# A transformer step whose last expert pair reaches the output sums through a one-hot product on TensorE

## What is computed

```python
def hier_moe(h, ...):
    ...
    g_idx = jnp.argmax(glog, axis=-1)              # 1 of 4 groups
    ...
    top_v, top_i = lax.top_k(elog_g, TOP_K)        # 2 of its 8 experts
    gate = jax.nn.softmax(top_v, axis=-1) * g_w[:, None]
    ...
    # expert e: (silu(x @ w_gate[e]) * (x @ w_up[e])) @ w_down[e], D 1024, FF 512
...
x = x + hier_moe(rms_norm(x, lw["ln_ffn"]), ...)
...
y_prompt = rms_norm(yp, final_norm_g)
y_sample = rms_norm(ys, final_norm_g)
```

## Time and profile before

| | us |
|---|---|
| median of three runs | 1164.77 |
| lowest, highest | 1164.1, 1165.12 |
| the profiled execution | 1165.38 |
| its span (first to last instruction) | 1163.6 |
| PE busy in it | 1032.4 |
| DVE, ACT, POOL busy | 458.5, 186.1, 113.1 |

### The profile page before, as it was taken

How to read it: one execution, slowest core, us unless ns; L and a number is a source line. 1 busy time by engine, 2 the same in 40 slices (tenths; PEclk the granted TensorE clock), 3 DMA queues, 4 the chain that set the end, 5 groups by cost and what they waited for, 6 DMA issues and landing times.

```text
span 1163.6 us, 11497 instructions
## 1 busy us (share of the span) xinstructions
PE 1032.4 (89%) x4528; PEld 540.7 (46%) x4528; DVE 458.5 (39%) x770; ACT 186.1 (16%) x486; POOL 113.1 (10%) x167
## 2 busy tenths in 40 slices
PE   6999999999999999999998699987876889887880
PEld 3577744555445446777656343333332233333320
DVE  4169645563664024013227743322222233322224
ACT  0156233433113101012101000000000000000001
POOL 1200001132016000000000010010000000100002
PEclk9999999999999999999998699999989899989995
DMA  8221130312233433212085599999999999999977
GB/s 254 73 73 54 45 123 1 134 52 82 74 108 103 177 145 145 73 57 89 1 355 200 220 397 427 427 427 426 428 427 426 422 427 427 426 427 427 413 297 251
DMA packets 56548, 277.50 MB, mean 238 GB/s; under 512 B 13360, under 2 KB 15280, under 8 KB 44336
## 3 DMA queue, kind: packets, MB, share of 16 engines
q1 hardware_dynamic: 43648, 256.01, 54.7%
q10 hardware_dynamic: 7808, 11.32, 2.7%
q0 software_dynamic: 5040, 9.45, 2.2%
HBM read 273.34 MB, written 18.61 MB: 251 GB/s over the span
## 4 chain that ended last, share of the span: by engine, by line
PE 69%; DMA 18%; DVE 6%; SPq 4%; issue 2%; ACT 0%; POOL 0%; ACTq 0%; DVEq 0%; POOLq 0%
PE bank L497 23%; DMA arena<-in_exp_w_down_dram 15%; PE bank L485 13%; PE bank L882 12%; PE bank L872 6%; SPq L1089 4%; PE bank L501 2%; PE bank L747 2%; PE score_pair L721 2%; PE bank L635 1%; DVE arena L1675 1%; DMA arena<-expert_rows 1%; PE score_pair L551 1%; PE bank L585 1%; DMA arena<-in_w_in_dram 1%
## 5 line engine op out<-in xcount | busy, mean ns | idle before, releaser
L497 PE MATMUL bank<-arena 128*128 128x512 f32 x640 | 285.0, 599 | 2.6 <-DMA arena<-in_w_in_dram 1.9
L882 PE MATMUL bank<-arena 128*64 128x512 f32 x1024 | 238.3, 622 | 38.5 <-issue 35.2
L497 PEld LDWEIGHTS bank<-arena 128*128 128x128 f32 x640 | 119.7, 191 | 147.0 <-issue 145.5
L882 PEld LDWEIGHTS bank<-arena 128*64 128x64 f32 x1024 | 83.4, 143 | 190.6 <-issue 189.4
L485 PE MATMUL bank<-arena 128*128 128x288 f32 x640 | 156.1, 406 | 0.0
L872 PE MATMUL bank<-arena 128*64 128x512 f32 x512 | 119.5, 621 | 26.6 <-DMA arena<-in_exp_w_down_dram 19.5
L485 PEld LDWEIGHTS bank<-arena 128*128 128x128 f32 x640 | 121.4, 190 | 33.8 <-issue 0.4
L1298 ACT ACTIVATE arena<-bank 128x512 f32<-128x512 f32 (+6 forms) x135 | 61.7, 493 | 378.3 <-PE bank L497 112.5
L872 PEld LDWEIGHTS bank<-arena 128*64 128x64 f32 x512 | 39.9, 142 | 95.1 <-issue 83.5
L1521 ACT ACTIVATE arena<-bank,arena 128x512 f32<-128x512 f32 x17 | 11.7, 687 | 428.3 <-PE bank L882 404.4
L2045 DVE SCALAR_TENSOR_TENSOR arena<-bank,arena 128x512 f32<-128x512 f32 x34 | 25.5, 751 | 109.8 <-PE bank L872 102.8
(11 more groups left out here) (295 smaller groups left out, 928.1 us busy)
## 6 DMA issues: line engine op xcount, KB each, us to landing
arena<-in_exp_w_gate_dram SPq DMA_DIRECT2D x30, 2048.0 KB, 33.0
arena<-in_exp_w_up_dram SPq DMA_DIRECT2D x30, 2048.0 KB, 37.7
arena<-in_exp_w_down_dram SPq DMA_DIRECT2D x28, 2048.0 KB, 34.7
arena<-in_w_in_dram SPq DMA_DIRECT2D x7, 2048.0 KB, 8.5
out_dram<-arena SPq DMA_DIRECT2D x4, 1024.0 KB, 10.5
arena<-in_w_mem_k_dram SPq DMA_DIRECT2D x2, 2048.0 KB, 10.3
arena<-in_w_mem_v_dram SPq DMA_DIRECT2D x2, 2048.0 KB, 8.6
arena<-in_w_out_dram SPq DMA_DIRECT2D x2, 2048.0 KB, 12.7
```

Source lines behind the costliest of these rows:

```text
L497: ins = mm(b[:, :], x, w[:, k, :], start=k == 0, stop=k == KC - 1)
L882: ins = mm(bank[own, :], xgT[:, k, own], w[j][:, k, :], start=k == 0, stop=k == KC - 1)
```

## The change

- POOL's scatter of the last pair (15) is gone. In its place POOL writes the numbers 0 to 575 into every partition (`iota`).
- DVE keeps for each slot of the last pair its token number (`last_tok`), and ahead of pair 15's drains compares the numbers with it: `hot_last`, 128 slots x 576 tokens, is 1 where the slot belongs to the token. It does not tell first from second expert.
- PE sums in PSUM. `place_last` multiplies `hot_last` of a tile by the drained rows of the last pair, which puts each row at its token; `add_loaded` adds the two loaded rows of each token by products with the identity. There are two banks for each tile (`summed`), the fifth tile taking those of the first again.
- ACT's square and DVE's scaling read these banks; DVE's sum is gone.
- The rows of `y_dram` that belong to slots of the last pair are no longer written, so all of `y_dram` is zeroed at the start: SP waits for POOL's constants and writes it from the zeroed `Vbd` in four DMAs, and `spread_v(0)` waits for them.
- SP issues all ten row loads, behind the final gain, and waits only for the scatters up to pair 14. ACT issues none. `yg` moves to parts that pair 15 does not use.

```diff
@@ -114,7 +114,8 @@
         ints = ctx.enter_context(nc.sbuf_tensor("ints", [P, 256], I32))
-        banks = [ctx.enter_context(nc.psum_tensor(f"bank{i}", [P, 512], F32)) for i in range(6)]
+        bank_pairs = [ctx.enter_context(nc.psum_tensor(f"banks{2 * i}", [P, 2, 512], F32)) for i in range(3)]
+        banks = [bank_pairs[i // 2][:, i % 2, :] for i in range(6)]
         pair = ctx.enter_context(nc.psum_tensor("score_pair", [P, 2, 512], F32))
@@ -216,7 +217,11 @@
-        yg = [[area(1024 * (2 * t + k), 1024) for k in range(2)] for t in range(NT)]
+        ROWS = 28672
+        yg = [[area(ROWS + 1024 * (2 * t + k), 1024) for k in range(2)] for t in range(NT)]
+        count_i = area(ROWS + 10240, TOK, dt=I32)
+        count = area(ROWS + 10240 + TOK, TOK)
+        hot_last = area(ROWS + 10240 + 2 * TOK, TOK)
         gfin = xg[1]
@@ -337,6 +342,7 @@
         ocol = fixed(4)
+        last_tok = fixed(1)
@@ -403,11 +409,14 @@
         over_done = sem("over_passes_done")
+        y_zero, count_ready, hot_last_ready = sem("y_rows_zeroed"), sem("token_count_ready"), sem("last_one_hot_ready")
+        f_full = sem("tokens_summed")
         gf_ld = sem("final_gain_loaded")
         yg_ld = [sem(f"y_rows_loaded{t}") for t in range(NT)]
-        fsum, fssq, frstd, fin_ready = (sem(f"final_{n}") for n in ("sum", "ssq", "rstd", "ready"))
+        fssq, frstd, fin_ready = (sem(f"final_{n}") for n in ("ssq", "rstd", "ready"))
         fin_st = sem("final_stored")
+        summed = [bank_pairs[0], pair, bank_pairs[1], bank_pairs[2], bank_pairs[0]]
         A = PsumRing(banks[0:3], a_full, a_free)
@@ -978,6 +987,37 @@
                     turn_rows(SP_, xg_rows[(i + 1) % 3])
+            pe.wait_ge(hot_last_ready, 1)
+
+            def place_last(t, half):
+
+                t0, rows = TILES[t]
+                mm(summed[t][0:rows, half, :], hot_last[:, t0:t0 + rows], yS[(PAIRS - 1) % 2][:, 512 * half:512 * (half + 1)],
+                   start=True, stop=False, skip_group_check=True)
+
+            def add_loaded(t):
+
+                rows = TILES[t][1]
+                pe.wait_ge(yg_ld[t], 32)
+                for half in range(2):
+                    for k in range(2):
+                        ins = mm(summed[t][0:rows, half, :], ident[0:rows, 0:rows], yg[t][k][0:rows, 512 * half:512 * (half + 1)],
+                                 start=False, stop=k == 1, skip_group_check=True)
+                ins.then_inc(f_full, 1)
+
+            for half in range(2):
+                pe.wait_ge(SP_.y_cp, 2 * PAIRS - 1 + half)
+                for t in range(2):
+                    place_last(t, half)
+            for t in range(2, SAMPLE):
+                for half in range(2):
+                    place_last(t, half)
+            for t in range(SAMPLE):
+                add_loaded(t)
+            pe.wait_ge(fin_ready, 1)
+            for half in range(2):
+                place_last(SAMPLE, half)
+            add_loaded(SAMPLE)
@@ -1004,6 +1044,10 @@
             sp.dma_start(cvN, a["cache_diff_v"][0, 0].rearrange("t h d -> t (h d)")).then_inc(ldcache, 16)
+            sp.wait_ge(pool_c, 2)
+            y_flat = y_dram.rearrange("(p r) n -> p (r n)", p=P)
+            for c in range(4):
+                sp.dma_start(y_flat[:, 2304 * c:2304 * (c + 1)], area(OZ, 2304)).then_inc(y_zero, 16)
             for u in range(2, 6):
@@ -1114,9 +1158,10 @@
             sp.wait_ge(y_st[0], 16 * (PAIRS // 2))
-            sp.wait_ge(y_st[1], 16 * (PAIRS // 2))
+            sp.wait_ge(y_st[1], 16 * (PAIRS // 2 - 1))
             for t, (t0, rows) in enumerate(TILES):
-                sp.dma_start(yg[t][0][0:rows, :], y_dram[t0:t0 + rows, :]).then_inc(yg_ld[t], 16)
+                for k in range(2):
+                    sp.dma_start(yg[t][k][0:rows, :], y_dram[TOK * k + t0:TOK * k + t0 + rows, :]).then_inc(yg_ld[t], 16)
             for t, (t0, rows) in enumerate(TILES):
@@ -1171,6 +1216,7 @@
                 if h == 0:
+                    po.wait_ge(y_zero, 64)
                     po.wait_ge(a_free, mark["proj", 5, SAMPLE])
@@ -1246,6 +1292,9 @@
             for i in range(PAIRS):
+                if i == PAIRS - 1:
+                    g.iota(count_i, pattern=[[1, TOK]], base=0, channel_multiplier=0).then_inc(count_ready, 1)
+                    break
                 po.wait_ge(SP_.y_cp, 2 * i + 2)
@@ -1545,13 +1594,10 @@
                     over_loop(act, over_pair)
-            act.wait_ge(y_st[0], 16 * (PAIRS // 2))
-            act.wait_ge(y_st[1], 16 * (PAIRS // 2))
-            for t, (t0, rows) in enumerate(TILES):
-                act.dma_start(yg[t][1][0:rows, :], y_dram[TOK + t0:TOK + t0 + rows, :]).then_inc(yg_ld[t], 16)
             for t, (_, rows) in enumerate(TILES):
-                act.wait_ge(fsum, t + 1)
-                f(yg[t][1][0:rows, :], yg[t][0][0:rows, :], ACT.Square, accum_out=ssq[0:rows, 17 + t:18 + t]).then_inc(fssq, 1)
+                act.wait_ge(f_full, t + 1)
+                f(yg[t][1][0:rows, :].rearrange("p (h n) -> p h n", h=2), summed[t][0:rows, :, :], ACT.Square,
+                  accum_out=ssq[0:rows, 17 + t:18 + t]).then_inc(fssq, 1)
@@ -2062,6 +2108,7 @@
                 n.step(ts(from_row[:, 0:NB // 2], got[:, 0], float(NOROW), None, ALU.add))
+                n.step(ts(last_tok, got[:, 0, PAIRS - 1:PAIRS], float(NOROW), None, ALU.add))
                 n.step(ts(table[:, 2], got[:, 1], float(TOK), float(NOROW), ALU.mult, ALU.add))
@@ -2100,6 +2147,10 @@
                     ve.wait_ge(gi_ready, over_total)
+                if i == PAIRS - 1:
+                    ve.wait_ge(count_ready, 1)
+                    n.link(v.tensor_copy(count, count_i))
+                    ts(hot_last, count, last_tok, None, ALU.is_equal).then_inc(hot_last_ready, 1)
                 drain_rows(SP_, i, 0, yS[i % 2], xg[i % 3], xm_ready, table[:, 3, i:i + 1])
@@ -2114,18 +2165,11 @@
             ve.wait_ge(gf_ld, 16)
-            for t in range(NT + 1):
-                if t < NT:
-                    rows = TILES[t][1]
-                    o = yg[t][0][0:rows, :]
-                    ve.wait_ge(yg_ld[t], 32)
-                    tt(o, o, yg[t][1][0:rows, :], ALU.add).then_inc(fsum, 1)
-                if t >= 1:
-                    rows = TILES[t - 1][1]
-                    o = yg[t - 1][0][0:rows, :]
-                    ve.wait_ge(frstd, t)
-                    stt(out=o, in0=o, scalar=rstd[0:rows, 16 + t:17 + t], in1=gfin[0:rows, :], op0=ALU.mult,
-                        op1=ALU.mult).then_inc(fin_ready, 1)
+            for t, (_, rows) in enumerate(TILES):
+                ve.wait_ge(frstd, t + 1)
+                stt(out=yg[t][0][0:rows, :].rearrange("p (h n) -> p h n", h=2), in0=summed[t][0:rows, :, :],
+                    scalar=rstd[0:rows, 17 + t:18 + t], in1=gfin[0:rows, :].rearrange("p (h n) -> p h n", h=2), op0=ALU.mult,
+                    op1=ALU.mult).then_inc(fin_ready, 1)
```

## The result

| | before | after |
|---|---|---|
| median, us (8 runs each, same chip) | 1164.51 | 1168.62 |
| lowest, highest | 1163.26, 1165.66 | 1167.63, 1169.73 |
| the profiled execution | 1165.38 | 1169.73 |
| its span | 1163.6 | 1168.0 |
| PE busy in it | 1032.4 | 1062.5 |

The changed kernel takes 1.0037 times as long, 95% interval 1.0026 to 1.0047: 4.1 us slower by the medians, where 3.1 were forecast (1167.9). The profiled execution of after is the longest of its eight, 1.1 us above their median, which matters when its times are set beside the forecast.

A forecast was written before the change was run, and what follows sets the result against it. Weights bound the kernel until 1131.8, then a tail, in which PE's 26.1 us replace 22.4 of scatter, loads and sums, with 0.5 back on POOL: +3.1 us. Added to the median, 1164.77 + 3.1 = 1167.9; range 1165.3 to 1171.5.

The forecast's parts named there:

- PE becomes the bound, and its price: Tail: thirty 512-column products at 0.859 us each, 25.8 us on PE, without a gap once started.
- D: PE tail: identity or one-hot products cost what transposes do, 0.545 us; tail 9.4 us shorter, 1158.5; chance 0.05.
- rival C: Sample tile: its six 64 x 64 products cost half, 2.6 us come back, 1165.3; chance 0.07.
- The start of the block: PE's products start 0.05 us after the drain of half 0, at 1133.86.
- The end: After the last sum: square and POOL 2.13 us, scaling 1.28, store and end 3.39.
- Reading PSUM: ACT's square and DVE's scaling in the tail: reading from PSUM put at nothing.
- The sum: Whole span: 1159.9 + 2.13 + 1.28 + 3.39 = 1166.7 against 1163.6, +3.1 us.
- rival B: Tail: the clock falls; at 1.2 GHz throughout it is 25.8 us longer, 1193.7; chance 0.03.
- rival E: Tail's fill, drain and store together 0.8 to 2 us shorter, 1165.9 to 1167.1; chance 0.09.
- Cast and compare: DVE ahead of the last drains: 1.5 us of work inside 6.91 us of idle time, costing nothing.
- they would not delay the weights: Row loads queued behind the last weights: taken as 0, bound 0 to +3 us.
- rival A: Row loads slow the last weights, 0.5 to 3 us more, 1168.4 to 1170.9; sign: block after 1134.5; chance 0.10.

The follow-up runs named there:

- e3_sum_pairs_on_dve: After, but DVE adds the two loaded rows and PE multiplies only their sum by the identity, twenty products: 1160.65 us, 0.9969 of before.
- e6_no_placing: After without all thirty PE products (last pair's rows missing from the output), DVE adding the two loaded rows: 1157.97 us, 0.994 of before.
- a_again: After, unedited, run once more: 1168.08 us, 1.0032 of before.
- e2_loads_behind_weights: After, but SP holds the ten row loads back until the last down weights have landed: 1167.75 us, 1.0031 of before.
- e1_zero_only: Before plus only the zeroing of the row buffer and POOL's wait for it: 1164.32 us, 0.9997 of before.
- e5_mix3: After, but DVE sums all loaded rows and adds placed rows for tiles 0, 1; PE adds for tiles 2, 3, 4: 1158.28 us, 0.9944 of before.
- e8_sample_on_pe: As e5_mix3, but PE adds both loaded rows of the sample tile, four products in place of two: 1159.32 us, 0.9954 of before.
- e4_place_only: After, but PE only places (ten products) and DVE does all the adding: 1160.69 us, 0.9965 of before.
- e5_mix2: As e4_place_only, but PE adds for tiles 3 and 4, DVE for tiles 0, 1 and 2: 1160.92 us, 0.9966 of before.
- e7_mix3_sum_first: As e5_mix3, but DVE sums the sample tile's loaded rows before scaling tile 1: 1158.18 us, 0.9947 of before.

## Why the prediction was right

**PE becomes the bound, and its price.** This is the step on which it rested, and it held to the hundredth: 3.43 for four products in the chain of after, 6.87 for eight, 0.859 each, as in the earlier trace rows. The whole block up to ACT's last square took 26.3 us (1134.89 to 1161.21) against 26.0 forecast (1133.86 to 1159.9). `e3_sum_pairs_on_dve` and `e6_no_placing` show it from the other side, by taking ten and thirty products away. The Trainium skill, "TensorE: Matmul & The Clock Gate", back-to-back issue gap, gives about 131 ns for each 512-column matmul in a sustained stream and 216 in isolation. Here a stream of f32 products took 0.859 = 4 x 0.215, the isolated figure four times; the measurement decides, and the rival that leaned on the other one (D) is out. Its threshold was a little high: at 0.75 us per product after would only break even with before, and to be faster by the 2.3 us that can be told it would need 0.68.

**The sample tile** (rival C) is not half price: its six products took 1.86 + 3.59 = 5.45 with the fill of the last one, where six at 0.859 and a fill of 0.16 are 5.31. The 0.14 between lies in the first two (1.86 for 1.72).

**The start of the block.** Forecast 0.05 after the drain of half 0; it took 0.14 ("issue" in the chain). And the first product, with nothing ahead of it to hide its beginning, has 1.10 in the chain, 0.24 above the price: that was no term of the sum and should have been one.

**The end.** From ACT's start on the last square to DVE's scaling 2.11 (forecast 2.13), scaling 1.27 (1.28), the end 1168.0 - 1164.59 = 3.41 (3.39). Reading PSUM cost nothing, as taken: the square 1.02 for 1.06 from SBUF.

**The sum.** Forecast for the tail: 1166.7 - 1133.06 = 33.6; measured 34.0, in `a_again` and `e2_loads_behind_weights` too. The missing 0.4 are 0.09 and 0.24 at the start and 0.14 at the sample tile, less 0.09 at ACT (0.03 for the 0.12 taken). So the change costs 3.5 us in the tail (34.0 - 30.5), not 3.1. The clock stood at 1.00 through it (rival B), and neither end was shorter (rival E).

**What was to cost nothing** did, but for 0.2 us. Zeroing: `e1_zero_only`. Cast and compare: 0.45 + 0.52 under PE's product, the estimate had been 1.5. The loads themselves: `e2_loads_behind_weights`. That they would not delay the weights was the weakest of these steps, since it was worked out from two rates and put at 0. It was nearly so: the last down quarter comes 10.2 us behind the last up quarter with the loads queued, and 10.0 without. The two rates, 394 and 407 GB/s per full share, had been read as equal; they are 3% apart, and 3% of the last 8 us of the weights is an estimate of 0.2 us. The Trainium skill, "DMA: Bandwidth & Descriptors", queues, rings and completion order, has descriptors taken in ring order on each engine. That agrees: 4.7 MB behind the weights go with 0.2 us of delay.

**Where the profile departs from what was said would show it.** The block started at 1134.89, later than the 1134.5 that was to mean rival A. By that test alone A would have been taken as shown, and wrongly: PE did not wait for weights, its down product ran at 0.50 for part of its length. The mark was an absolute time, and two causes lead to it; the row that tells them apart is the wait before the last quarter, or the clock.

**What stays open** is this fall of the clock between 1124 and 1130. It is in the profiles of after and of `e2_loads_behind_weights`, `e3_sum_pairs_on_dve`, `e6_no_placing`, `e5_mix3` and `e8_sample_on_pe`, and absent from those of before, `e1_zero_only`, `a_again`, `e4_place_only`, `e5_mix2` and `e7_mix3_sum_first`. The gaps ahead of it, 0.92 and 0.78 us, are the same in all. Its price can be told: from the start of the down product to the start of the drains it is 8.04 to 8.05 us in the six with the fall, 6.98 to 7.05 in the four others with the change (6.85 and 6.82 without it), so about 1.0. Since the same kernel has it in one execution and not in the other, it does not come with the kernel alone. But both profiles of kernels without the change lack it, and two are too few to say that the change does not make it more likely. In the two profiles of after the drains start at 1134.00 and at 1132.29; 1.0 of these 1.7 us is the fall, and the rest lies ahead of the down product. The two comparisons of medians, 4.1 and 3.4 us, stand on both sides of the 3.7 that the tail and the late weights make. Their intervals, 3.0 to 5.5 and 2.2 to 5.1, would leave room for the 0.6 on average that six falls in ten executions would cost.

## What to carry to other kernels

Moving a sum of f32 rows onto TensorE is not free just because the engine was idle: each 512-column product stands 0.86 us in a row with the others, and five tiles of six products are more than the scatter and the loads that they replace. Count the new engine's row from end to end before the old chain is taken out, and give each engine only as much as leaves them level, as `e5_mix3` does. And do not leave TensorE idle just before its last work: in the profiled execution of `e5_mix2` the slow clock after a gap of 4 us cost 3.8 (7.38 for 3.60), and the two products that it saved are worth 1.7.

## What was not expected of the hardware

- A gap of 3.99 us on PE was followed by 0.50 of the clock for all of the next four products, 7.38 us for 3.60, though DVE was at work throughout the gap. The earlier trace rows had shown it after 4.22 us; here it makes the version with fewer products on PE the slower one in the profiles.
- Gaps of 0.92 and 0.78 us were followed by a fall of the clock in six profiles and by none in another six.
- With ten row loads queued behind them the last weights came 0.2 us later (10.2 for 10.0 us), though the loads kept the DMA engines at a share of 1.02 where it had been 0.42 (1125 to 1130).
- POOL's second step over one column took 0.54 with DVE idle and 1.41 with a two-input op of DVE beside it (`e6_no_placing`), which makes two instructions over 128 values the longest link of that ring.
